# Second block's token shift: on-chip transfers in place of products with shifted unit matrices

## The reference, cut to what matters

```python
def token_shift(z, mu_prev, mu_next):
    z_prev = jnp.pad(z, ((0, 0), (1, 0), (0, 0)))[:, :-1]
    z_next = jnp.pad(z, ((0, 0), (0, 1), (0, 0)))[:, 1:]
    return z + mu_prev * (z_prev - z) + mu_next * (z_next - z)

z = h @ w_in                                  # (256, 3328)
qa, ka, va = z[..., :512], z[..., 512:1024], z[..., 1024:1536]
zr = token_shift(z[..., 1536:], mu_prev, mu_next)
r, k, v = zr[..., 0:512], zr[..., 512:1024], zr[..., 1024:1536]
xw, xa, xg = zr[..., 1536:1600], zr[..., 1600:1664], zr[..., 1664:1792]
# xw, xa, xg -> small products -> decay, a, g; k -> kk; then the recurrence over the 256 tokens
```

## Time and profile before

| | before |
|---|---|
| runs: median (lowest to highest) | 4131.65 us (4130.72 to 4133.0), 3 runs |
| profiled execution: own time / span | 4129.21 us / 4127.4 us |
| mean granted PE clock | 0.888 of full speed |
| PE busy over the span | 3286.8 us (80%) |
| DVE busy | 2551.3 us (62%) |
| ACT busy | 1078.8 us (26%) |
| POOL busy | 1543.4 us (37%) |
| mean rate of all transfers | 322 GB/s |

### The profile page before, as it was taken

One profiled execution on the slowest core, in us unless ns is written; L12 is line 12 of the kernel. 1 busy time (PEld: TensorE's weight loads), 2 busy tenths in 40 slices (PEclk: granted clock), 3 DMA queues, 4 the chain that ended last, 5 costly groups with the idle time before them and its releaser, 6 DMA issues.

```text
span 4127.4 us, 36789 instructions
## 1 busy us (share of the span) xinstructions
PE 3286.8 (80%) x11238; PEld 1688.2 (41%) x11238; DVE 2551.3 (62%) x5418; ACT 1078.8 (26%) x2926; POOL 1543.4 (37%) x1636
## 2 busy tenths in 40 slices
PE   6889797898878788886688875667878888897776
PEld 2348552456434334551245421222356655442111
DVE  1321768566787956677445784866573344877777
ACT  1321111321211122121223332433232112333333
POOL 0110466655566767666103332323000002333332
PEclk9999899999979999996899998786889999999666
DMA  6573799999999999999849999999500026999998
GB/s 235 205 264 143 282 399 388 365 378 412 402 405 400 393 364 409 411 409 407 302 160 388 368 398 410 406 410 413 187 10 1 1 94 254 406 394 412 420 420 370
DMA packets 307067, 1330.34 MB, mean 322 GB/s; under 512 B 31308, under 2 KB 36684, under 8 KB 237752
## 3 DMA queue, kind: packets, MB, share of 16 engines
q0 software_dynamic: 239616, 1141.06, 69.8%
q1 hardware_dynamic: 61104, 164.18, 10.6%
q10 hardware_dynamic: 6152, 22.74, 1.5%
HBM read 1326.69 MB, written 1.17 MB: 322 GB/s over the span
## 4 chain that ended last, share of the span: by engine, by line
PE 19%; DMA 17%; DVE 11%; issue 3%; ACT 2%; ACTq 0%; DVEq 0%; POOL 0%; POOLq 0%
PE ps L1754 18%; DMA arena<-in_peer_rows,arena 16%; DVE arena L915 4%; DVE arena L928 3%; ACT arena L2537 2%; PE ps L1760 1%; DMA arena<-in_ada_w 1%; DVE arena L936 1%; DVE arena L1304 1%; DVE arena L1309 1%; DVE ps L928 1%; DVE arena L1299 0%; DVE arena L1320 0%; DMA arena<-in_peer_up,arena 0%; DVE arena L1314 0%
## 5 line engine op out<-in xcount | busy, mean ns | idle before, releaser
L1754 PE MATMUL ps<-arena 128*128 128x512 f32 (+9 forms) x10500 | 3187.3, 484 | 734.0 <-ACT arena L2537 408.8
L1754 PEld LDWEIGHTS ps<-arena 128*128 128x128 f32 (+4 forms) x10500 | 1596.7, 194 | 2247.4 <-issue 1795.0
L928 DVE SCALAR_TENSOR_TENSOR arena<-arena,ps 128x1024 f32<-128x1024 f32 x1024 | 1239.3, 1216 | 544.6 <-DMA arena<-in_peer_rows,arena 351.4
L2537 ACT ACTIVATE arena<-arena 128x1 f32<-128x1 f32 (+3 forms) x2240 | 705.9, 326 | 1580.9 <-DVE arena L928 849.4
L3202 POOL DMA_INDIRECT arena<-in_peer_rows,arena x512 | 492.9, 963 | 1516.7 <-DVE arena L932 627.2
L3202 POOL DMA_INDIRECT arena<-in_peer_down,arena x512 | 489.6, 956 | 433.8 <-DVE arena L932 196.8
L3202 POOL DMA_INDIRECT arena<-in_peer_up,arena x512 | 494.4, 966 | 292.4 <-PE ps L1754 177.3
L2537 ACT ACTIVATE arena<-ps 128x512 f32<-128x512 f32 (+4 forms) x349 | 191.0, 547 | 990.1 <-PE ps L1754 677.4
L928 DVE SCALAR_TENSOR_TENSOR ps<-arena,ps 128x512 f32<-128x512 f32 x508 | 382.2, 752 | 72.2 <-DMA arena<-in_peer_up,arena 66.5
L915 DVE TENSOR_TENSOR arena<-ps,arena 128x512 f32<-128x512 f32 (+3 forms) x192 | 131.3, 684 | 250.3 <-PE ps L1754 222.2
L915 DVE TENSOR_TENSOR arena<-arena 128x512 f32<-128x512 f32 (+8 forms) x366 | 241.2, 659 | 41.6 <-ACT arena L2537 21.1
(11 more groups left out here) (33 smaller groups left out, 502.7 us busy)
## 6 DMA issues: line engine op xcount, KB each, us to landing
arena<-in_w_mod POOLq DMA_DIRECT2D x40, 1024.0 KB, 7.4
arena<-in_gate_blocks SPq DMA_DIRECT2D x16, 2048.0 KB, 10.6
arena<-in_w_in SPq DMA_DIRECT2D x14, 2048.0 KB, 23.3
arena<-in_w_pq SPq DMA_DIRECT2D x13, 2048.0 KB, 19.6
arena<-in_ada_w POOLq DMA_DIRECT2D x24, 1024.0 KB, 7.8
arena<-in_w_out SPq DMA_DIRECT2D x8, 2048.0 KB, 11.5
arena<-in_gate_blocks SPq DMA_DIRECT2D x8, 1792.0 KB, 10.1
arena<-mod_scratch ACTq DMA_DIRECT2D x26, 512.0 KB, 9.5
```

The costliest lines, as they stand in the source:

```text
L928: self.e.scalar_tensor_tensor(o, a, s, b, op0, op1, accum_out=accum).then_inc(*(inc or self.inc(self.S.vec)))
L1754: return self.e.matmul(o, l, r, start=start, stop=stop)
L2537: self.e.activation(o, i, f, bias=bias, scale=scale, accum_out=accum).then_inc(*(inc or self.inc(self.S.act)))
```

## The change

PE has no part in the shift any more. After the evictions of both tiles of block j, ACT issues six transfers inside the on-chip memory: rows 0 to 111 of both tiles one row further into a buffer `PREV`, rows 1 to 112 one row back into `NEXT`, the remaining 15 rows each way, and the two single rows that cross from one tile to the other. ACT waits before them until DVE has read the last shift's `PREV` and `NEXT` (there is one pair of buffers). DVE waits for all six (semaphore `shift_in`, 96) and does 5 operations on both tiles at once, 128 x 2 x 512 numbers each. The rows outside the sequence are zeroed once per execution, by `shift_edges`, two memsets between the end of the gather and `second_norm(1)`; the filling of `K.edges` is dropped.

```diff
@@ main
         self.fence()
         self.slot, self.ring = self.slots["three"], self.rings["wide"]
+        self.shift_edges()
         self.run(self.second_norm(1))
@@ Vector.second_vectors
         self.wait_ge(*sh_in)
-        self.memset(K.edges, 0.0)
-        self.copy(K.edges[:, 0:1], K.ident[:, 127:128])
-        self.copy(K.edges[:, 255:256], K.ident[:, 0:1])
@@ Vector
+    def shift_edges(self):
+        self.memset(self.K.PREV[0:1, 0, :], 0.0)
+        self.memset(self.K.NEXT[:, 1, :], 0.0, inc=self.inc(self.S.edges))
@@ Vector.shift
         r = slice(o - 1536, o - 1536 + n)
-        banks = [self.bank() for _ in range(4)]
-        for t in range(2):
-            self.wait_ge(*self.full(banks[2 * t + 1]))
-            z, a, c = K.Z2[:, t, o:o + n], K.QN[:, 0:n], K.KN[:, 0:n]
-            bp, bn = banks[2 * t], banks[2 * t + 1]
-            self.tt(a, bp.ap[:, 0:n], K.MU[:, 0, r], M, inc=self.drain(bp))
-            self.tt(c, bn.ap[:, 0:n], K.MU[:, 1, r], M, inc=self.drain(bn))
-            self.tt(a, a, c, AD)
-            self.wait_ge(*self.full(banks[3]))
-            self.tt(z, z, K.STAY[:, r], M)
-            self.tt(z, z, a, AD, inc=self.inc(self.S.shifted) if j == 6 and t else None)
+        wide = lambda a: a.unsqueeze(1).to_broadcast([128, 2, n])
+        z, p, c = K.Z2[:, :, o:o + n], K.PREV[:, :, 0:n], K.NEXT[:, :, 0:n]
+        self.wait_ge(*self.next(self.S.shift_in, 96))
+        self.tt(p, p, wide(K.MU[:, 0, r]), M)
+        self.tt(c, c, wide(K.MU[:, 1, r]), M)
+        self.tt(z, z, wide(K.STAY[:, r]), M)
+        self.tt(z, z, p, AD)
+        self.tt(z, z, c, AD, inc=self.inc(self.S.shifted) if j == 6 else None)
+        self.mark(("shift read", j))
@@ Tensor.shift
-        self.wait_ge(*self.drained(self.zs[1, j]))
-        for t in range(2):
-            z, other = K.Z2[:, t, o:o + n], K.Z2[:, 1 - t, o:o + n]
-            bp, bn = self.bank(), self.bank()
-            self.wait_ge(*self.vacant(bp))
-            ins = self.mm(bp.ap[:, 0:n], K.before, z, True, t == 0)
-            if t == 1:
-                ins = self.mm(bp.ap[:, 0:n], K.edges[:, 0:128], other, False, True)
...
@@ Scalar.shift
-        for _ in range(4):
-            self.bank()
+        z = K.Z2[:, :, o:o + n]
+        for t in range(2):
+            self.wait_ge(*K.marks["z", t, j])
+        if self.shifts:
+            self.wait_ge(*K.marks["shift read", self.shifts[-1]])
+        else:
+            self.wait_ge(*self.next(S.edges))
+        latest = self.latest
+        for a, b in ((0, 112), (112, 127)):
+            self.e.dma_start(K.PREV[a + 1:b + 1, :, 0:n], z[a:b]).then_inc(S.shift_in, 16)
+            self.e.dma_start(K.NEXT[a:b, :, 0:n], z[a + 1:b + 1]).then_inc(S.shift_in, 16)
+        self.e.dma_start(K.PREV[0:1, 1, 0:n], z[127:128, 0, :]).then_inc(S.shift_in, 16)
+        self.e.dma_start(K.NEXT[127:128, 0, 0:n], z[0:1, 1, :]).then_inc(S.shift_in, 16)
+        self.shifts.append(j)
+        self.latest = latest
@@ memory
+    shifted = Mem(arena, (ab, ab + 2048))
+    K.PREV, K.NEXT = shifted(2, 512), shifted(2, 512)
```

More of the change, by code:

```diff
@@ L151, in __init__ @@
         self.pair_uses = [0] * 9
-        self.zs = {}
+        self.zs, self.shifts = {}, []
         self.outs, self.turned_in, self.closed_in, self.wq = {}, {}, {}, {}
@@ L555, in second_vectors @@
         pass
+    def shift_edges(self):
+        pass
     def second_norm(self, t):
@@ L2271, in z_block @@
         yield
-    def shift(self, j):
-        K = self.K
-        n, o = (512, 512 * j) if j < 6 else (256, 3072)
-        self.wait_ge(*self.drained(self.zs[1, j]))
-        for t in range(2):
-            z, other = K.Z2[:, t, o:o + n], K.Z2[:, 1 - t, o:o + n]
-            bp, bn = self.bank(), self.bank()
-            self.wait_ge(*self.vacant(bp))
-            ins = self.mm(bp.ap[:, 0:n], K.before, z, True, t == 0)
-            if t == 1:
-                ins = self.mm(bp.ap[:, 0:n], K.edges[:, 0:128], other, False, True)
[L2285 to L2291, removed]
     def attend2(self):
@@ L2963, in z_block @@
         self.evict(b, self.K.Z2[:, t, 512 * j:512 * j + n], b.ap[:, 0:n])
+        self.mark(("z", t, j))
         yield
     def shift(self, j):
-        for _ in range(4):
-            self.bank()
+        K, S = self.K, self.S
+        n, o = (512, 512 * j) if j < 6 else (256, 3072)
+        z = K.Z2[:, :, o:o + n]
[13 more added lines that the diff above has]
+        self.latest = latest
         yield
@@ L3368, in memory @@
     K.ident, K.iota = K.K0[:, 16:144], K.K0[:, 144:160]
-    K.before, K.after = K.K0[:, 15:143], K.K0[:, 17:145]
     K.small = keep(64)
@@ L3425, in memory @@
     K.STAY = K.KE[:, 256:2048]
-    K.final_g, K.edges = K.H2[:, 2, :], K.H2[:, 3, 0:256]
+    K.final_g = K.H2[:, 2, :]
     K.MIX = K.H2[:, 2:4, :]
@@ L3490, in semaphores @@
     S.mu_in, S.second_in, S.rows_in, S.final_in, S.final_x = one("mu_in"), one("second_in"), one("rows_in"), one("final_in"), one("final_x")
-    S.shifted = one("shifted")
+    S.shifted, S.shift_in, S.edges = one("shifted"), one("shift_in"), one("edges")
     S.qk_mean, S.qk_root, S.qk_normed, S.prob2 = one("qk_mean"), one("qk_root"), one("qk_normed"), one("prob2")
```

## The result

| | before | after |
|---|---|---|
| median of 7 runs each, us | 4131.65 | 4146.26 |
| lowest to highest, us | 4126.23 to 4139.93 | 4142.25 to 4149.14 |
| profiled execution: time and span, us | 4129.21 and 4127.4 | 4147.68 and 4145.9 |

After against before is 1.0034, with an interval of 1.0024 to 1.0044. The change made the kernel slower, by about 14 us. The forecast was 4132.6 us and no measurable change, with a range of 4129 to 4140. Forecast and range both missed.

The account below looks back on a forecast made before the run. The prediction took a chain through PE's products, then DVE operation after operation, as the bound. Shift delays and DVE savings netted +0.9 us on the 4131.65 median, giving 4132.6 us, range 4129 to 4140.

Parts of the forecast that it names:

- What the transfers take: Step pricing a shift's six on-chip transfers, 1020 KB, from two 512 KB loads of x: 5.5 us, bounds 4.0 and 8.0.
- L: Time of a shift's transfers from ACT's first issue to the last landing, taken as 5.5 us for every shift.
- The upper bound of 8.0: Ceiling on a shift's transfer time: a 2048 KB load's landing of 7.9 us, every byte counted twice, as read and written.
- The sum around it: Shift-by-shift addition of transfer times, DVE work and waits from block 4's eviction to the stage's end: +0.9 us.
- its own +0.9: Forecast net delay in us at the end of the stage that holds the shifts, with transfers of 5.5 us.
- the three shifts on the path: Shifts 6, 4 and 3, one behind the other: 1 us more per shift's transfers adds 3 us to the sum.
- The landings are long: Slower rival: transfers of 7.5 us or more in ACT's queue ahead of DVE, 4140 to 4142 us; 12 in 100.
- its counter-argument: Against long landings: DMA share in 2975 to 2990 is 0.08, so transfers have the engines almost alone.
- the rival that the clock stays low: Slower rival: PE at 1.2 GHz throughout block 1 and `decays(1)`, +7 to +14, 4139 to 4146 us; 3 in 100.
- PE was the price: Faster rival: DVE's waits go with PE's products, with shorter DVE work about -16, 4115 us; 4 in 100.
- the prediction's own signs of being wrong: Landing over 7.5 us after first issue, wide operations well above 1.23, DVE awaiting PE at `decays(1)`, or differences outside 2944 to 3026.

Follow-up runs that it names:

- e5: Changed kernel with 32 KB loads in place of the 2 MB weight loads of blocks 0 and 2 for tile 1; 4134.81 us (a single run).
- e3: Changed kernel without the two 15-row transfers of each shift, DVE waiting for the four that remain; 4137.4 us (a single run).
- e8: Kernel before, PE still making the shifted rows, with DVE doing 5 wide operations on both tiles in place of 10; 4130.71 us, 1.0002 of before.
- e6: Changed kernel with SP issuing the transfers in place of ACT, each shift ahead of a weight load, one pair of buffers; 4125.83 us, 0.9989 of before.
- e7: As e6, with a second pair of buffers and a second semaphore, so the next shift is fetched while one is read; 4123.23 us, 0.9984 of before.
- e9: As e7, with SP's order changed to load of block 5, shift 6, shift 4, load of block 0 and on; 4119.49 us, 0.9968 of before.
- e1: Changed kernel with SP's weight loads of blocks 0 and 2 held until DVE has read shifts 6 and 3; 4145.4 us, 1.0037 of before.
- e4: Changed kernel with the 112 and 15 rows sent as one transfer of 127 rows, four transfers a shift; 4292.22 us (a single run).

## Why the prediction was wrong

**The step that failed is "What the transfers take".** L = 5.5 was the price of two large loads issued at 0.42 us, set on six transfers, four of them small and all of them in the way of one another. Without the loads of blocks 0 and 2, L was 5.84, 6.77, 7.06 and 6.79 (e5). For 4.7 to 5.4 us of these ACT was issuing, for which 2.7 were allowed; the row used for the small ones (0.23 us) was that of other transfers, to another place. The Trainium skill ("DMA: Bandwidth & Descriptors", Anatomy of one DMA) gave the estimate of 4.4 us for a shift's bytes as one transfer that GpSimd issues. No run here has such a transfer on chip, and the six that ACT issues took 6.7 in shift 4. With a load beside them L was 10.92 (shift 6) and 10.21 (shift 3). The prediction named the load that shift 6 meets and set against it only that this shift has half the bytes; the load that shift 3 meets it did not expect. The upper bound of 8.0 did not hold either: it counted a shift's own bytes twice and no bytes of others.

**The sum around it held.** With the measured L in the prediction's own formula: its own +0.9, then L above 5.5 for the three shifts on the path (5.42 + 1.22 + 4.71 = 11.35), then 0.63 for shift 5, which is no longer hidden, then 0.95 for DVE's waits for PE at `decays(1)` (0.44 and three of 0.17). That makes 13.8, and the stage grew by 13.84. The same for e5 gives 0.9 + (0.34 + 1.27 + 1.56) + 0.59 + 1.45 = 6.1, and 6.07 was measured. Split by the runs, 7.8 of the 13.84 is contention with the two loads, about 3.8 the issues and landings above 5.5 without it, 0.9 the prediction's own, and the rest waits for PE. How the 3.8 divide between issues and landings was not separated.

**The rival that happened had 12 in 100.** "The landings are long" had the right place (ACT's queue ahead of DVE), at 4140 to 4142, 4 us short. Its reasons (small transfers behind large ones, one pair of buffers) are at most the smaller part; the larger, contention with the loads, is what its counter-argument ruled out. That argument was the DMA share of 0.08 in 2975 to 2990. That stretch is of the kernel before, where block 2's load went out at 2987.75, after shift 3. The change itself moves this load forward, for it frees PE and with it the slot, and moves the shift back. The share had to be read for the order after the change, not before. Over how many engines the 15 rows go no run shows. Their 60 KB landed in 3.9 us at the median, with 4.2 for 448 KB, and leaving them out shortened shift 4 by 1.0 (e3).

**What was right.** The wide operations took 1.226 us each (five in 6.27), and by e8 they win nothing by themselves. The two memsets of `shift_edges`, 0.48 us each, lie under ACT's square: what follows them came 0.07 later, counted from the end of the gather. `decays(0)` no longer waits for PE. PE idles twice, for 10.00 us before block 5 and 23.32 before block 1 (4 and 15 were forecast; most of the surplus follows from the longer L), and its clock comes back within the products of block 1. DVE waited only 0.95 us for PE at `decays(1)`, so the rival that the clock stays low did not happen, nor did "PE was the price": in after, PE's busy time fell by 13 us (18 were forecast, at the full clock) and the kernel became slower. Two of the prediction's own signs of being wrong were there: landings more than 7.5 us after the first issue, and that wait for PE at `decays(1)`.

## What to carry to other kernels

A DMA share read before a change speaks of the order before it: ask which loads the change sets free earlier, and whether they will meet the new transfers on the engines. Price a group of transfers by the queue's issue time as well, one by one and by place: six issues took some 5 us here, and the last transfer can't land before its own issue. If transfers replace products, issue them from a queue where no unrelated work stands ahead of them, and put large loads that are needed later behind them: the same six transfers then gained 0.1 to 0.3% here (e6, e7 and e9, the last two with a second pair of buffers) instead of losing 0.34%.

## What the runs showed of the hardware

- An issue's time depends on what stands ahead of it in the queue and on what runs beside it. A single row of 2 KB took 0.61 us to issue in the fifth place (after) and 1.28 to 1.31 in the third and fourth, behind two transfers of 448 KB (e3). With a 2 MB load beside them the fifth and sixth issues took 1.47 to 1.67 (e1, shifts 4 and 5). That ACT waits there for room in its queue is how this reads; it was not shown by itself.
- On-chip transfers lose to a 2 MB load on another queue: 8.3 us against 2.9 to land 224 KB (after, e5), and 10.2 to 11.0 (after, e1) against 5.8 to 7.1 (e5) for a whole shift. Issued ahead of the load in the same queue, so that it went out after them, they landed in 2.9 (e6).
- Transfers of 127 rows moved 24 GB/s at a DMA share of 0.07, and an issue behind one of 508 KB took 13 to 23 us (e4).
